# The search stage of a hybrid attention block: stores in two transfers, three query buffers, masks in five steps, another order

## What is computed

```python
proj = einsum('bsd,de->bse', rmsnorm(x, g1) * (1 + sc1) + sh1, w_in)     # 3280 columns
rel = relu(einsum('bqhd,bkd->bqhk', q_idx, k_idx))                        # 16 heads of 64
score = where(chunk_allowed(q_pos, k_pos), einsum('bqh,bqhk->bqk', w_idx, rel), -inf)
top_val, top_idx = top_k(score, 256)                                      # keys attended by 8 heads
```

## Time and profile before

| | us |
|---|---|
| median of 3 runs | 3533.34 |
| lowest and highest run | 3532.78, 3537.93 |
| span of the profiled execution, first to last instruction | 3528.7 |
| `index_projection` | 0 to 291 |
| `indexing` | 294 to 1036 |
| values, attention, MLP | 1040 to 3529 |

### The profile page before, as it was taken

How to read it: one execution, slowest core, us unless ns; L and a number is a source line. 1 busy time by engine, 2 the same in 40 slices (tenths; PEclk the granted TensorE clock), 3 DMA queues, 4 the chain that set the end, 5 groups by cost and what they waited for, 6 DMA issues and landing times. The chain is left out here.

```text
span 3528.7 us, 44735 instructions
## 1 busy us (share of the span) xinstructions
PE 3215.3 (91%) x15808; PEld 2589.9 (73%) x15808; DVE 2505.4 (71%) x4762; ACT 1860.6 (53%) x3101; POOL 427.3 (12%) x690
## 2 busy tenths in 40 slices
PE   5998988988987889989889989999989999999998
PEld 4787767876755666767667778778878878888787
DVE  6444788888875676777868667878788775665676
ACT  4313777877766778878787633432242223222232
POOL 0011122101200000000000000022112120000231
PEclk9999999999985999989999999999999999999999
DMA  6575433323336432211211236354444445664555
GB/s 226 165 234 139 116 104 101 89 69 99 108 123 160 109 93 50 49 47 41 54 25 37 73 127 216 129 190 141 157 162 150 154 175 195 244 224 167 195 214 199
DMA packets 330637, 471.76 MB, mean 134 GB/s; under 512 B 25328, under 2 KB 217024, under 8 KB 330032
## 3 DMA queue, kind: packets, MB, share of 16 engines
q1 hardware_dynamic: 280576, 305.09, 28.8%
q0 software_dynamic: 49840, 163.83, 13.7%
HBM read 311.84 MB, written 156.98 MB: 133 GB/s over the span
## 5 line engine op out<-in xcount | busy, mean ns | idle before, releaser
L2363 PE MATMUL m_ps<-m_h,w_hi 128*128 128x512 f32 x1792 | 558.1, 393 | 19.5 <-DVE w_lo L1965 10.3
L2363 PEld LDWEIGHTS m_ps<-m_h,w_hi 128*128 128x128 f32 x1792 | 337.8, 189 | 95.4 <-DVE w_lo L1965 15.9
L921 PE MATMUL isps<-ki,iq 128*128 128x512 f32 (+3 forms) x1216 | 308.1, 389 | 69.5 <-ACT spare L951 51.8
L1029 DVE SCALAR_TENSOR_TENSOR rank<-spare,iw,rank 128x1024 f32<-128x1024 f32 (+5 forms) x330 | 329.8, 1021 | 58.1 <-ACT spare L951 53.9
L2376 PE MATMUL m_ps<-w_hi,a_hi 128*128 128x512 f32 x896 | 350.1, 391 | 6.3 <-DVE w_lo L2194 3.4
L2363 PE MATMUL m_ps<-m_h,w_lo 128*128 128x512 f32 x896 | 350.9, 392 | 0.0
L2376 PE MATMUL m_ps<-w_lo,a_hi 128*128 128x512 f32 x896 | 349.9, 390 | 0.0
L2376 PE MATMUL m_ps<-w_hi,a_lo 128*128 128x512 f32 x896 | 349.7, 390 | 0.0
L921 PEld LDWEIGHTS isps<-ki,iq 128*128 128x128 f32 x1216 | 231.2, 198 | 144.7 <-issue 39.2
L951 ACT ACTIVATE spare<-isps 128x1024 f32<-128x1024 f32 (+5 forms) x352 | 276.7, 818 | 65.8 <-PE isps L921 51.5
L2861 PE MATMUL tps<-ident,probs 128*128 128x128 f32 x1632 | 240.4, 290 | 58.2 <-DVE probs L3077 54.7
(11 more groups left out here) (294 smaller groups left out, 6646.0 us busy)
## 6 DMA issues: line engine op xcount, KB each, us to landing
w_raw<-in_w_ff SPq DMA_DIRECT2D x136, 512.0 KB, 5.4
dram_aop<-a_out POOLq DMA_DIRECT2D x224, 256.0 KB, 2.6
a_lo<-dram_aop SPq DMA_DIRECT2D x56, 1024.0 KB, 5.4
queries<-dram_proj SPq DMA_DIRECT2D x128, 256.0 KB, 4.3
iq<-dram_proj SPq DMA_DIRECT2D x224, 128.0 KB, 3.0
ada_w<-in_w_ada POOLq DMA_DIRECT2D x16, 1024.0 KB, 6.6
dram_proj<-r_ev_hi POOLq DMA_DIRECT2D x104, 128.0 KB, 2.7
dram_proj<-r_ev_lo POOLq DMA_DIRECT2D x104, 128.0 KB, 2.8
```

What stands on the lines that cost most here:

```text
L921: mm = nc.tensor.matmul(sps[:, job.n % 2, a:b], iq[:, job.unit % IQU, job.head % 2, part, :], ki[:, job.c * SCH + a:job.c * SCH + b], star ...
L1029: nc.vector.scalar_tensor_tensor(out=dst, in0=got, scalar=w, in1=dst, op0=ALU.mult, op1=ALU.add).then_inc(s_acc, 1)
L2363: mm = nc.tensor.matmul(ps[:, b], w[:, w1_slot(n, j), k, :], hop[:, j, h, :, k, :], start=fresh and k == 0 and i == 0, stop=k == KH - 1 an ...
```

## The change

- The projection in HBM becomes [tile, high or low, 128, 2048]; each part of a unit is stored by one transfer of 128 rows (two instead of four). `head_rows` reads one head from it; the loads of queries, keys and values in all stages use the new places with the same contiguous pieces of 512 B or more.
- In the search stage the high part is stored once ACT has written it, the low part once DVE has; each of the four buffers has a semaphore. ACT waits before it writes a high buffer for its store and for DVE's reading; DVE waits before it writes a low buffer for its store. Low buffers alternate by the count of low parts (`n_lo`).
- `IQU`, the buffers of queries, goes from 2 to 3 (also in the view of `load_unit` and in the matmul's index, not shown).
- The mask is five steps of the plan, each beginning with a wait for the step before; POOL stores it after the last (`part == 4`). The step that writes `tie` comes after the mask before.
- The plan: assumed durations, keys, slack and allowances for loads are others, and a store takes `STORE` = 3.5 in it.

```diff
@@ -57,10 +57,10 @@
 PT = 3
-INDEX_LATENCY, INDEX_SLACK = 0.15, 0.12
-REST_FROM, REST_PACE, REST_LOAD, ROUNDS = 102.09, 1.0, 9.0, 0.2
-INDEX_PLACES = dict(evac=50.6, evac_lo=49.92, relu=-1.01, mm=-1.08, index=-1.64, add=0.48, chain0=0.58, lo=-0.51, chain1=0.76,
-                    keep=-1.78, split=-1.67)
+INDEX_LATENCY, INDEX_SLACK = 0.15, 0.02
+REST_FROM, REST_PACE, REST_LOAD, ROUNDS = 3495.99, 10.15, 9.0, 0.35
+INDEX_PLACES = dict(evac=766.13, evac_lo=-1281.15, relu=-475.21, mm=-1248.76, index=-610.35, add=325.32,
+                    chain0=-23.36, lo=397.39, chain1=-22.66, keep=1254.42, split=-543.2)
 ATT_LATENCY, ATT_SLACK = 0.15, 0.07
@@ -83,7 +83,7 @@
-        self.proj = t("proj", [CT * P // DH, 2, DH, SEQ])
+        self.proj = t("proj", [CT, 2, P, SEQ])
         self.gates = t("gates", [2, DM])
@@ -93,6 +93,12 @@
         self.w2_sums = t("w2_sums", [2, FF // 2, DM // 2])
+def head_rows(scr, row):
+    at = row // DH % 2 * DH
+    return scr.proj[row // P, :, at:at + DH, :]
@@ -307,9 +313,8 @@
                     for part, src in enumerate((ev_hi, ev_lo)):
-                        for half in range(2):
-                            sp.dma_start(scr.proj[INDEX_TILES[i] * P // DH + half, part, :, g * GT:(g + 1) * GT],
-                                         src[half * DH:(half + 1) * DH, n % EV, :].bitcast(F32)).then_inc(s_st[n % EV], 16)
+                        sp.dma_start(scr.proj[INDEX_TILES[i], part, :, g * GT:(g + 1) * GT],
+                                     src[:, n % EV, :].bitcast(F32)).then_inc(s_st[n % EV], 16)
                 sp.wait_ge(s_gr, 1)
@@ -327,7 +332,7 @@
                     if n >= EV:
-                        act.wait_ge(s_st[n % EV], 64 * (n // EV))
+                        act.wait_ge(s_st[n % EV], 32 * (n // EV))
                     if INDEX_TILES[order[n][0]] == CT - 1:
@@ -658,10 +663,10 @@
                 key = k + h / I_HEADS
-                score = put("index", Step("score", "PE", 0.03 + 0.91 * width / SCH, key, [], **more))
-                relu = put("relu", Step("relu", "ACT", 0.09 + 0.84 * width / SCH, key, [score], **more))
+                score = put("index", Step("score", "PE", 0.06 + 0.86 * width / SCH, key, [], **more))
+                relu = put("relu", Step("relu", "ACT", 0.06 + 0.87 * width / SCH, key, [score], **more))
                 score.of = relu
-                add = put("add", Step("add", "DVE", 0.15 + 1.07 * width / SCH, key,
+                add = put("add", Step("add", "DVE", 0.13 + 1.07 * width / SCH, key,
                                       [relu] + (freed[k - 3:k - 2] if k >= 3 else []), **more))
@@ -673,11 +678,15 @@
             where = k + 1 + ROUNDS * r / TOPK_ROUNDS
-            last = put(chain, Step("count", "ACT" if on_act else "DVE", (0.36 if on_act else 0.2) + (0.86 if on_act else 1.08) * size,
+            last = put(chain, Step("count", "ACT" if on_act else "DVE", (0.34 if on_act else 0.2) + (0.83 if on_act else 1.08) * size,
                                    where, [last], block=b, k=k, r=r, on_act=on_act))
-            last = put(chain, Step("judge", "DVE", 0.4, where, [last], block=b, k=k, r=r, on_act=on_act,
+            last = put(chain, Step("judge", "DVE", 0.36, where, [last], block=b, k=k, r=r, on_act=on_act,
                                    last=(r + 1) % 8 == 7))
-        freed.append(put(chain, Step("mask", "DVE", 1.2 + 6.6 * size, k + 1 + ROUNDS, [last], block=b, k=k)))
+        for part, cost in enumerate((0.95 + 1.08 * size, 0.25 + 1.05 * size, 0.05 + 2.08 * size, 0.05 + 1.06 * size,
+                                     0.05 + 1.06 * size)):
+            last = put(chain, Step("mask", "DVE", cost, k + 1 + ROUNDS,
+                                   [last] + ([freed[-1]] if part == 1 and freed else []), block=b, k=k, part=part))
+        freed.append(last)
     units = []
@@ -693,13 +702,15 @@
                                     tile=tile, g=g, part=k, n=m))
-            evac = put("evac", Step("evac", "ACT", 0.6, where, [mm] + ([units[m - 2].of] if m >= 2 else []),
+            evac = put("evac", Step("evac", "ACT", 0.59, where, [mm] + ([units[m - 2].of] if m >= 2 else []),
                                     tile=tile, g=g, n=m))
+            evac.stored = streams["evac"][m - 2] if m >= 2 else None
             mm.of = evac
...
                 n_lo += 1
-                mm.of = put("evac_lo", Step("evac_lo", "DVE", 0.7, where, [evac], tile=tile, g=g, n=m))
+                mm.of = put("evac_lo", Step("evac_lo", "DVE", 0.67, where, [evac], tile=tile, g=g, n=m))
                 mm.of.n_lo = n_lo
+                mm.of.stored = streams["evac_lo"][n_lo - 3] if n_lo >= 3 else None
             units.append(mm)
@@ -719,7 +730,7 @@
                 after.append(streams["relu"][job.n - 2])
-            t = unit_end.get(job.unit - IQU, FIRST_LOADS) + 3.0
+            t = unit_end.get(job.unit - IQU, FIRST_LOADS) + QUERY_LOAD
         elif job.kind == "split" and job.n == 1:
@@ -729,6 +740,10 @@
             after.append(streams["add"][job.n - 2])
+        elif job.stored is not None:
+            if job.stored.end is None:
+                return None
+            t = job.stored.end + STORE
         for other in after:
@@ -775,7 +790,6 @@
     evacs = streams["evac"]
-    stores = [sum(1 if e.tile in FULL_TILES else 4 for e in evacs[:n + 1] if e.n % 2 == n % 2) for n in range(len(evacs))]
     with ExitStack() as ctx:
@@ -819,7 +833,8 @@
         s_elo = sem("s_rest_evac_lo")
-        s_st = [sem(f"s_rest_stored{n}") for n in range(2)]
+        s_st = [sem(f"s_rest_hi_stored{n}") for n in range(2)]
+        s_lst = [sem(f"s_rest_lo_stored{n}") for n in range(2)]
         s_sc = sem("s_rest_scales")
@@ -832,17 +847,16 @@
                         sp.wait_ge(s_qk, units[n - IQU][2])
-                    row = R_IQ // DH + head
-                    view = scr.proj[row:row + 2, :, :, b * P:(b + 1) * P].rearrange("m r p q -> p (m r) q")
+                    view = scr.proj[(R_IQ + head * DH) // P, :, :, b * P:(b + 1) * P].rearrange("r (m p) q -> p (r m) q", p=DH)
                     for half in range(2):
-                        sp.dma_start(iq[half * DH:(half + 1) * DH, n % IQU].rearrange("p m r q -> p (m r) q").bitcast(F32),
+                        sp.dma_start(iq[half * DH:(half + 1) * DH, n % IQU].rearrange("p r m q -> p (r m) q").bitcast(F32),
                                      view).then_inc(s_q[n % IQU], 16)
...
                 load_unit(0)
-                sp.dma_start(ki[:].bitcast(F32), scr.proj[R_IK // DH].rearrange("r p t -> (r p) t")).then_inc(s_k, 16)
+                sp.dma_start(ki[:].bitcast(F32), head_rows(scr, R_IK)).then_inc(s_k, 16)
                 for part, dst in enumerate(iw_rows):
-                    sp.dma_start(dst, scr.proj[R_IW // DH, part, 0:I_HEADS, 2 * P:SEQ]).then_inc(s_iwt, 16)
+                    sp.dma_start(dst, head_rows(scr, R_IW)[part, 0:I_HEADS, 2 * P:SEQ]).then_inc(s_iwt, 16)
                 for n in range(1, len(units)):
@@ -855,24 +869,19 @@
                 load_w(1)
-                stored = [0, 0]
                 kept = [0, 0, 0]
                 for job in plan:
-                    if job.kind == "evac" and job.tile in FULL_TILES:
+                    tokens = slice(job.g * GT, (job.g + 1) * GT) if job.kind in ("evac", "evac_lo") else None
+                    if job.kind == "evac":
                         pool.wait_ge(s_ehi, job.n + 1)
                         row = (job.tile - FULL_TILES[0]) * P
-                        pool.dma_start(scr.av[row:row + P, job.g * GT:(job.g + 1) * GT],
-                                       ev_hi[:, job.n % 2, :].bitcast(F32)).then_inc(s_st[job.n % 2], 16)
-                        stored[job.n % 2] += 1
+                        dst = scr.av[row:row + P, tokens] if job.tile in FULL_TILES else scr.proj[job.tile, 0, :, tokens]
+                        pool.dma_start(dst, ev_hi[:, job.n % 2, :].bitcast(F32)).then_inc(s_st[job.n % 2], 16)
                     elif job.kind == "evac_lo":
                         pool.wait_ge(s_elo, job.n_lo)
-                        for part, src in enumerate((ev_hi, ev_lo)):
-                            for half in range(2):
-                                pool.dma_start(scr.proj[job.tile * P // DH + half, part, :, job.g * GT:(job.g + 1) * GT],
-                                               src[half * DH:(half + 1) * DH, job.n % 2, :].bitcast(F32)
-                                               ).then_inc(s_st[job.n % 2], 16)
-                        stored[job.n % 2] += 4
-                    elif job.kind == "mask":
+                        pool.dma_start(scr.proj[job.tile, 1, :, tokens],
+                                       ev_lo[:, job.n_lo % 2, :].bitcast(F32)).then_inc(s_lst[job.n_lo % 2], 16)
+                    elif job.kind == "mask" and job.part == 4:
                         pool.wait_ge(s_mask, job.k + 1)
@@ -966,7 +976,9 @@
                         if job.n >= 2:
```

(47 more changed lines are left out.)

37 lines of the change are left out of this document (20 added, 17 removed).

## The result

The changed kernel takes 3563.4 us (4 runs, 3561.7 to 3564.6) against 3535.6 us of the kernel before on the same chip: the ratio is 1.0076, with a 95% interval of 1.0061 to 1.0090. It is slower by 0.8%, where 1.6% faster was forecast.

A forecast was written before the change was run, and what follows sets the result against it. In the search stage no engine was taken to be full: they wait for one another. Terms of 38 + 10 + 6 + 0 + 1 = 55 us off 3533.3 gave 3478 us, range 3445 to 3520.

The forecast's parts named there:

- the one on the rest of the kernel: Outside the search stage: attention reads the same 512 B pieces from other places, gain nothing; the stage before gains 1 us.
- the one on the slow side: Rival, search stage: high-part stores stuck in POOL's order hold ScalarE; 25 us slower, 3558 us, chance 0.07.
- VectorE's low part: Rival, search stage: ScalarE's evacuations wait for VectorE's low part instead of the DMA; about 20 us gained, 3513, chance 0.20.
- the clock: TensorE in the search stage: less idling may give back part of 29 us lost at half clock; put to nothing.
- One sign: Search stage: if the forecast is right, no wait of TensorE over 5 us is seen beside a mask.
- Stores, 38 us: Search stage: earlier, merged stores remove 60 of ScalarE's 70 us of waits, worth 38 us, bounds 25 and 60.
- Masks, 10 us: Search stage: masks in five steps let other work go between them; 10 us gained, bounds nothing and 20.
- Query buffers, 6 us: Search stage: a third buffer removes 14 of TensorE's 15.9 us of query waits; half counts, 6 us, bounds 0 and 16.
- Order, 0: Search stage: ready chain steps always go before adds; own effect taken as nothing, bounds -15 and +20 us.
- the doubled size costs nothing: Search stage's merged stores: 256 KB lands in 2.8 us like 128 KB, so no added latency and an issue saved.

The follow-up runs named there:

- keys_by_part: The changed kernel with each load of keys, in search and attention, as two transfers of 64 rows instead of one: 3464.8 us, ratio 0.9809 to the kernel before.
- keys_interleaved: The changed kernel with key loads' source as [64, 2, n], high and low rows interleaved over partitions, queries placed to match: 3451.8 us, ratio 0.9777 to the kernel before.
- plan_without_stores: keys_interleaved with a plan that takes a store to need no time, all waits in the kernel kept: 3477.9 us, ratio 0.9845 to the kernel before.
- five_steps_old_rest: The kernel before with key rows interleaved over partitions and masks in five steps, nothing else of the change: ratio 0.9989, against 0.9969 without the five steps.

## Why the prediction was wrong

**The step that failed** is the one on the rest of the kernel: "The attention stage reads the same 512 B pieces from other places: nothing." It looked at the size of the pieces and at the queries, and took the loads of keys to be the same as well. Their bytes and pieces are the same; their outermost dimension went from 128 to 2, and that cost 11 to 17 us at the search's start and 83 us in attention, 94 us in all by the ratios and 99 by the medians (3563 against 3465). Of the 83 us some 40 came after attention's first score, where TensorE hardly waited for loads, but ScalarE stood 42 us longer for output stores on POOL's queue. No rival held it either: the one on the slow side was POOL's queue, and in the search stage POOL did nothing of the kind. The diff showed both lines that load keys, the search's and attention's; the forecast has no price for either, although nine loads of keys stand on SP's queue ahead of the first score of attention, because it counted bytes and pieces and not dimensions.

**What was right.** Without that, the change gives 3465 us (keys_by_part) where 3478 was forecast, within the range of 3445 to 3520. The search stage takes 658 us (670 forecast), counted from its late start; the waits for stores went from 70 to 0 (10 forecast), for queries from 15.9 to 2.9 (2). VectorE is busy 587 of 658 us, as the 595 of the earlier trace rows had it. VectorE's low part hardly became a new wait (1.0 us of ScalarE, 2.8 of TensorE), and POOL issues 104 stores in place of 208. POOL still stands for masks, 39.3 us with a longest wait of 12.5, but no wait of ScalarE for a store comes of it. TensorE is busy 626 us instead of 650, at a clock of 0.97 instead of 0.96; the forecast had put the clock to nothing, and what this is worth in time no run parts from the rest.

One sign failed: that TensorE would not wait over 5 us beside a mask. At 628.9 it has waited 8.1 us for a relu. VectorE worked on a mask's steps from 616.5 to 626.1, with a count of its own among them, and ScalarE's count waited 6.2 us for the judge behind it:

```profile
628.91 2.48 PE L931 MATMUL isps<-ki,iq 128*128 128x512 f32 x6 [8.09 <-ACT spare L961]
```

**Sizes, by parts.** The sum was nearly right (67 us by the ratio of keys_by_part, 55 forecast), its terms were not; that their errors made up for one another is luck. The terms below, most of them measured by undoing one part, don't add up to the whole either: 14, 14, 65 and 40 us come to 133, where keys_interleaved gains 79.
- Stores, 38 us: 14 by undoing them in the new order, 17 by adding only the early store to the old one. What the plan knows of them, taken away, costs 24 us, but not through waits for stores (2.1 us), so it can't be added.
- Masks, 10 us: 7 us lost when added alone, 65 lost when taken away from the new order. Both runs end on projection that was left over, so neither prices the steps. The mechanism is in the trace in part: the longest wait of TensorE for a relu goes from 11.5 to 5.7 us when they are added alone, from 12.3 to 8.1 in the new order.
- Query buffers, 6 us: 14, known to 8. TensorE's 11.5 us of waits seem to count in full here, not by half.
- Order, 0 (between a loss of 15 and a gain of 20): 40 by undoing it. It was bounded by what was left of VectorE's idle time, not by the end of the stage. There the runs differ: before, the projection's last matmul started at 997 and the last score at 1032, with the new order at 937 and 967; in the four runs that undo or add one part of the plan the projection comes last, 16 to 40 us after the last score. So the 40 us are what the old priorities lose under the new plan. What the new ones win in the old kernel was not run.
- Of the merged stores I said that the doubled size costs nothing. They land in 3.2 us, the halves had landed in 2.7 and 2.8. The Trainium skill (DMA: Bandwidth & Descriptors, "Anatomy of one DMA"), whose 0.3 us for the doubled bytes I set aside, has the sign right; the size no run tells, since the same transfers land in 2.8 to 3.3 us from run to run (2.8 and 2.9 in plan_without_stores). It cost next to nothing, even where the plan made no room for a store: 2.1 us of ScalarE's waits in plan_without_stores.

```profile
dram_proj<-r_ev_hi POOLq DMA_DIRECT2D x52, 256.0 KB, 3.2
dram_proj<-r_ev_lo POOLq DMA_DIRECT2D x52, 256.0 KB, 3.2
```

## What to carry to other kernels

When a change moves a tensor in HBM, list every transfer that reads it, in all stages, and write down the dimensions of both sides after merging. Here an outermost 2 in place of 128 brought the share of the DMA engines down to 0.13; what stood behind it on the issuing queue came later, and stores of another queue landed later too. If a dimension of 2 has to be there, put it second, and let the partitions carry the permutation. When an order is worked out by a program with tuned priorities, undoing one part measures that part plus the lost balance, so the same part should also be added alone to the old kernel. That can lose the balance as well (five_steps_old_rest), so look in both which job of the stage ends last.

## What the runs showed of the hardware

- A 256 KB load with source [2, 64, 512] takes some 4.4 us of SP's time to issue when several follow one another, against 0.53 with 128 rows and 0.6 to 0.7 with [64, 2, 512], and 0.51 when it comes singly; query loads, mask loads and further keys behind it on the same queue slow down with it (4 us for a pair of query loads instead of 1.3). While such loads move alone the DMA share is 0.13 of 16 engines, at 49 GB/s. Stores that POOL issues meanwhile land late (64 KB in 5.7 us, before 1.9).
- The same 128 or 256 KB of queries into every second partition lands in 2.7 and 3.4 us, into 64 neighbouring partitions in 3.0 and 4.3 us (medians). With the keys interleaved to match, the kernel before is 0.3% faster (0.9969, 0.9956 to 0.9981). Why it is so, no run here tells.
